# A hybrid decoder trunk on one core: gated-delta and mLSTM outputs gated by halves of the heads, weight splits moved at the starts of the feed-forward blocks

## The reference

```python
x = x + 0.5 * _rmsnorm(_swiglu(_rmsnorm(x, ng[0]), w_ffn_up[layer, 0], w_ffn_down[layer, 0]), ng[1])
h = _rmsnorm(x, ng[2])
... # h = mixer(h)
x = x + _rmsnorm(h, ng[3])
x = x + 0.5 * _rmsnorm(_swiglu(_rmsnorm(x, ng[4]), w_ffn_up[layer, 1], w_ffn_down[layer, 1]), ng[5])
```

```python
o = _rmsnorm(o, norm_w) * jax.nn.silu(z.astype(f32).reshape(B, T, GDN_HEADS, GDN_DV))   # gated delta
y = o.reshape(B, T, GDN_Z).astype(x.dtype) @ w_out
...
h = h * jax.nn.sigmoid(o.astype(f32).reshape(B, T, ML_HEADS, ML_DV))                    # mLSTM
y = h.reshape(B, T, ML_V).astype(x.dtype) @ w_out
```

## Time and profile before

| | us |
|---|---|
| median of 3 runs (lowest, highest) | 2773.89 (2772.54, 2776.75) |
| profiled execution | 2778.04 |
| its span from first to last instruction | 2776.4 |
| PE busy | 2669.9 |
| DVE, ACT, POOL busy | 1538.1, 1158.4, 287.1 |
| mean granted TensorE clock | 0.985 of full |

### The profile page before, as it was taken

One profiled execution on the slowest core, in us unless ns is written; L12 is line 12 of the kernel. 1 busy time (PEld: TensorE's weight loads), 2 busy tenths in 40 slices (PEclk: granted clock), 3 DMA queues, 4 the chain that ended last, 5 costly groups with the idle time before them and its releaser, 6 DMA issues.

```text
span 2776.4 us, 52143 instructions
## 1 busy us (share of the span) xinstructions
PE 2669.9 (96%) x22228; PEld 2518.8 (91%) x22228; DVE 1538.1 (55%) x1842; ACT 1158.4 (42%) x1571; POOL 287.1 (10%) x294
## 2 busy tenths in 40 slices
PE   7999999999999999999999999999999999999998
PEld 6998987899999986699999989699999989878998
DVE  4556744665555444465565553465455558446654
ACT  4434544444443344443344333344444335445442
POOL 1000004200200125110010000010020000042000
PEclk9999999999999999999999999999999999999999
DMA  6544522454554535444455453454455445135443
GB/s 189 164 139 147 155 81 71 152 166 146 171 166 138 194 113 160 143 146 162 144 171 166 140 177 117 126 161 163 146 169 169 141 147 166 61 99 159 153 144 101
DMA packets 415627, 404.26 MB, mean 146 GB/s; under 512 B 14786, under 2 KB 411950, under 8 KB 415086
## 3 DMA queue, kind: packets, MB, share of 16 engines
q1 hardware_dynamic: 411348, 397.42, 45.1%
q0 software_dynamic: 4096, 4.20, 0.5%
HBM read 385.19 MB, written 16.39 MB: 145 GB/s over the span
## 4 chain that ended last, share of the span: by engine, by line
PE 85%; DVE 10%; ACT 4%; issue 1%; DMA 0%; SPq 0%; ACTq 0%; DVEq 0%
PE psum L363 22%; PE psum L365 21%; PE psum L364 21%; DVE w_lo L345 2%; DVE x L574 1%; DVE y L572 1%; ACT w_hi L338 1%; PE psum L2679 1%; DVE g_cacc L1610 1%; PE psum L1150 1%; PE psum L1035 1%; PE psum L1167 1%; DVE xn_lo L499 1%; PE psum L2080 1%; PE psum L1036 1%
## 5 line engine op out<-in xcount | busy, mean ns | idle before, releaser
L345 DVE TENSOR_TENSOR w_lo<-raw,w_hi 128x2048 fp32r<-128x2048 f32 (+3 forms) x366 | 756.7, 2067 | 521.2 <-ACT w_hi L338 521.1
L363 PE MATMUL psum<-xn_hi,w_hi 128*128 128x288 f32 x3296 | 986.7, 299 | 29.9 <-DVE w_lo L345 19.1
L364 PE MATMUL psum<-xn_lo,w_hi 128*128 128x288 f32 x3296 | 977.0, 296 | 0.0
L365 PE MATMUL psum<-xn_hi,w_lo 128*128 128x288 f32 x3296 | 973.9, 295 | 0.0
L338 ACT ACTIVATE w_hi<-raw 128x2048 fp32r<-128x2048 f32 (+3 forms) x366 | 623.6, 1704 | 715.1 <-PE psum L365 672.4
L363 PEld LDWEIGHTS psum<-xn_hi,w_hi 128*128 128x128 f32 x3296 | 622.5, 189 | 41.4 <-issue 19.2
L365 PEld LDWEIGHTS psum<-xn_hi,w_lo 128*128 128x128 f32 x3296 | 625.2, 190 | 0.0
L364 PEld LDWEIGHTS psum<-xn_lo,w_hi 128*128 128x128 f32 x3296 | 623.4, 189 | 0.6
L364 PE MATMUL psum<-h_lo,w_hi 128*128 128x288 f32 x1408 | 415.5, 295 | 0.0
L363 PE MATMUL psum<-h_hi,w_hi 128*128 128x288 f32 x1408 | 415.0, 295 | 0.0
L365 PE MATMUL psum<-h_hi,w_lo 128*128 128x288 f32 x1408 | 414.9, 295 | 0.0
(11 more groups left out here) (566 smaller groups left out, 3073.3 us busy)
## 6 DMA issues: line engine op xcount, KB each, us to landing
raw<-w_ffn_up SPq DMA_DIRECT2D x176, 1024.0 KB, 5.1
raw<-w_ffn_down SPq DMA_DIRECT2D x64, 768.0 KB, 4.2
raw<-w_ffn_down SPq DMA_DIRECT2D x64, 640.0 KB, 3.9
...
```

Of the source, the lines that this page charges most:

```text
L345: dve.tensor_tensor(spread(w_lo[slot(u, i)], u), packed(raw[u % NRAW], u), spread(w_hi[slot(u, i)], u).bitcast(F32), ALU.subtract).then_in ...
L363: pe.matmul(out, wh[:, k, c], hi(k), start=st, stop=False)
L364: pe.matmul(out, wh[:, k, c], lo(k), start=False, stop=False)
L365: last = pe.matmul(out, wl[:, k, c], hi(k), start=False, stop=sp_)
```

## The change

Five edits, all of order, waits and counts; each arithmetic instruction is still there.

1. *Feed-forward start.* The split of the third unit goes ahead of the last square.
2. *Gated delta, end.* DVE gates, ACT rounds and DVE subtracts first the even parts (heads 0 to 3, chunks 0 to 3 of the projection), then the odd ones. The first unit of the projection is written out: both column halves over chunks 0 to 3, which wait for 3 `low`, then both over chunks 4 to 7, which wait for 6. The wait for `g_f` 6 is gone, and 13 fillers stand in place of 16.
3. *mLSTM, end.* The same by halves. Six updates in place of five go into the last two gate tiles, and none after them; four transposes stand ahead of the last tile and the fifth within it; three gates go between the last updates; 15 fillers are added; the copies to `nall` go behind the gates, and the transpose of `nall` and `nout` behind the first unit.
4. *mLSTM, end.* ACT waits only for the DMA of the first sample state (`l_c0_saved`), not for all four.
5. *mLSTM, start.* DVE splits the unit u0+4 within the chain of small instructions, ACT splits u0+5 ahead of its wait for that chain.

```diff
@@ act_pre_ffn
-                if k % 2 == 1:
+                if k % 2 == 1 and k < KC - 1:
                     act_square_x(act, n, k // 2)
+            act_split(act, ubase[n] + 2)
+            act_square_x(act, n, H - 1)
@@ act_ffn, pair
-                if not second:
+                if not first and not second:
                     act_split(act, u0 + 2 * j + 2, i)
@@ pe_gdn
-            pe_filled(pe, u0 + 17, 1, 16)
+            pe_filled(pe, u0 + 17, 1, 13)
             once(pe, "g_s_new", 8)
             once(pe, "g_s_odd", 8)
-            once(pe, "g_f", 6)
-            pe_out(pe, n, u0 + 17, xn(xn_hi), xn(xn_lo), lambda k: once(pe, "g_o_split", 5 + k // 4) if k % 4 == 0 else None)
+            pe.wait_ge(lo_ready, u0 + 18)
+            wh, wl = wview(w_hi[slot(u0 + 17)], u0 + 17), wview(w_lo[slot(u0 + 17)], u0 + 17)
+            for g in range(2):
+                once(pe, "g_o_split", 3 * g + 3)
+                for m in range(2):
+                    out, c = psum[:, m, 0:T], slice(m * P, (m + 1) * P)
+                    for k in range(4 * g, 4 * g + 4):
+                        pe.matmul(out, wh[:, k, c], xn_hi[:, k, :], start=k == 0, stop=False)
+                        pe.matmul(out, wh[:, k, c], xn_lo[:, k, :], start=False, stop=False)
+                        last = pe.matmul(out, wl[:, k, c], xn_hi[:, k, :], start=False, stop=k == KC - 1)
+            last.then_inc(unit_used, 1)
+            pe_out(pe, n, u0 + 17, xn(xn_hi), xn(xn_lo), None, first=1)
@@ act_gdn
-            for k in range(6):
+            for k in (0, 2, 4, 1, 3, 5):
                 hi(k)
@@ dve_gdn
             gated(0)
+            gated(2)
+            low(0)
+            gated(4)
+            low(2)
+            low(4)
             gated(1)
-            for k in range(2, 6):
-                low(k - 2)
-                gated(k)
-            low(4)
+            gated(3)
+            gated(5)
+            low(1)
+            low(3)
             low(5)
@@ sp_mlstm
-            once(sp, "l_c_out0", 64)
+            once(sp, "l_c0_saved", 16)
+            once(sp, "l_c_out0", 48)
@@ pe_mlstm
-            o_tile(pe, n, 6, range(20, 25))
-            ml_turned(pe, 0)
-            ml_turned(pe, 1)
-            o_tile(pe, n, 7, range(25, 32))
-            ml_turned(pe, 2)
-            ml_turned(pe, 3)
-            ml_turned(pe, 4)
+            o_tile(pe, n, 6, range(20, 26))
+            for k in range(4):
+                ml_turned(pe, k)
+            o_tile(pe, n, 7, range(26, 32))
+            once(pe, "l_f", 3)
+            pe_filled(pe, u0 + 13, 2, 15)
+            once(pe, "l_o_split", 3)
+            once(pe, "l_evac", 15)
...
+            last.then_inc(unit_used, 1)
             once(pe, "l_nall", 1)
-            once(pe, "l_evac", 16)
-            pe.transpose(psum[0:LH + NB * LH, 1, 0:P], nall[:], ident).then_inc(sem("l_n_turned"), 1)
-            once(pe, "l_n_out", 1)
+            pe.transpose(psum[0:LH + NB * LH, 7, 0:P], nall[:], ident).then_inc(sem("l_n_turned"), 1)
+            pe_out(pe, n, u0 + 13, xn(xn_hi), xn(xn_lo), None, first=1)
@@ act_mlstm
-                act_split(act, u0 + i + 2)
+                if i != 3:
+                    act_split(act, u0 + i + 2)
...
                 elif i == 2:
+                    act_split(act, u0 + 5)
                     once(act, "l_pre_rows", 1)
...
+            act.wait_ge(unit_used, u0 + 13)
+            for k in range(3):
+                high(k)
+            o_copy(7)
+            o_sigmoid(3)
+            for k in range(3, 6):
+                high(k)
+            once(act, "l_c0_saved", 16)
@@ dve_mlstm
                     dve.tensor_scalar(tmp4(3)[:, 0:1], tmp4(3)[:, 0:1], 0.0, None, ALU.max)
+                    dve_split(dve, u0 + 4)
                     step(dve.tensor_tensor(sq3(tmp4(3))[:, :, 0], sq3(tmp4(3))[:, :, 0], m0[:], ALU.max))
```

More of the change, by code:

```diff
@@ L575, in dve_update, with pe_out @@
             dve_enter(dve, n + 1, chunk)
-        def pe_out(pe, n, u0, hi, lo, ready):
-            for i in range(H):
+        def pe_out(pe, n, u0, hi, lo, ready, first=0):
+            for i in range(first, H):
+                if subs[n][0] == "mlstm" and i == H - 1:
+                    once(pe, "l_n_out", 1)
                 pe_unit(pe, u0 + i, [psum[:, 2 * i, 0:T], psum[:, 2 * i + 1, 0:T]], hi, lo, True, True,
@@ L1969, in pe_mlstm @@
                 ml_state(pe, h)
-            o_tile(pe, n, 6, range(20, 25))
-            ml_turned(pe, 0)
-            ml_turned(pe, 1)
-            o_tile(pe, n, 7, range(25, 32))
-            ml_turned(pe, 2)
-            ml_turned(pe, 3)
-            ml_turned(pe, 4)
+            o_tile(pe, n, 6, range(20, 26))
[6 more added lines that the diff above has]
+            once(pe, "l_evac", 15)
+            pe.wait_ge(lo_ready, u0 + 14)
+            wh, wl = wview(w_hi[slot(u0 + 13)], u0 + 13), wview(w_lo[slot(u0 + 13)], u0 + 13)
+            for g in range(2):
+                if g == 1:
+                    once(pe, "l_o_split", 6)
+                for m in range(2):
+                    if g == 0 and m == 1:
+                        once(pe, "l_evac", 16)
+                    out, c = psum[:, m, 0:T], slice(m * P, (m + 1) * P)
+                    for k in range(4 * g, 4 * g + 4):
+                        pe.matmul(out, wh[:, k, c], xn_hi[:, k, :], start=k == 0, stop=False)
+                        pe.matmul(out, wh[:, k, c], xn_lo[:, k, :], start=False, stop=False)
+                        last = pe.matmul(out, wl[:, k, c], xn_hi[:, k, :], start=False, stop=k == KC - 1)
+            last.then_inc(unit_used, 1)
             once(pe, "l_nall", 1)
-            once(pe, "l_evac", 16)
-            pe.transpose(psum[0:LH + NB * LH, 1, 0:P], nall[:], ident).then_inc(sem("l_n_turned"), 1)
-            once(pe, "l_n_out", 1)
-            pe_out(pe, n, u0 + 13, xn(xn_hi), xn(xn_lo), lambda k: once(pe, "l_o_split", 3 + 3 * (k // 4)) if k % 4 == 0 else None)
+            pe.transpose(psum[0:LH + NB * LH, 7, 0:P], nall[:], ident).then_inc(sem("l_n_turned"), 1)
+            pe_out(pe, n, u0 + 13, xn(xn_hi), xn(xn_lo), None, first=1)
         def ml_columns(pe):
@@ L2121, in ml_turned @@
             else:
-                once(pe, "l_c_new", NB * LH)
+                once(pe, "l_hs", 1)
+                once(pe, "l_f", 1)
                 for e in range(2):
-                    last = pe.transpose(psum[:, 6, tile(e)], Hs[:, tile(e)], ident)
+                    last = pe.transpose(psum[:, 4, tile(e)], Hs[:, tile(e)], ident)
             last.then_inc(sem("l_ot"), 1)
@@ L2206, in act_mlstm, with high @@
             o_copy(6)
-            o_copy(7)
-            o_sigmoid(3)
-            act.preload_act_table_set("natural_log_exp_and_others")
-            for k in range(6):
+            def high(k):
                 it, g = l_item(k)
@@ L2222, in act_mlstm @@
                 act_split(act, u0 + 13 + i + 1)
+                if i == 0:
+                    act.preload_act_table_set("natural_log_exp_and_others")
+                    once(act, "l_n_turned", 2)
+                    act.activation(nout[:], psum[0:LH + NB * LH, 7, 0:P], ACT.Copy).then_inc(sem("l_n_out"), 1)
                 act_square_y(act, n, i, u0 + 13 + i)
@@ L2338, in dve_mlstm @@
             dve_split(dve, u0 + 13)
[L2339 to L2346 removed]
+            smallT = psum[:, 4, 0:2 * P].rearrange("p (e h t) -> p h e t", e=2, h=LH)
             by_head = lambda v: v.rearrange("p (h e) t -> p h e t", e=2)
@@ L2366, in low @@
                                   ALU.subtract).then_inc(sem("l_o_split"), 1)
-            gated(0)
-            gated(1)
-            for k in range(2, 6):
-                low(k - 2)
+            updated(range(20, 26))
+            for k in range(3):
+                updated(range(26 + k, 27 + k))
                 gated(k)
-            low(4)
-            low(5)
+            updated(range(29, 32))
+            for k in range(3):
+                low(k)
+            for k in range(3, 6):
+                gated(k)
+            for k in range(3, 6):
+                low(k)
+            once(dve, "l_cpe", LH)
+            once(dve, "l_c_new", 32)
+            dve.tensor_copy(nall[:, 0:LH, None], Cp[:, :, LC:LC + 1])
+            for h in range(LH):
+                last = dve.tensor_copy(nall[:, LH:].rearrange("p (b h) -> p b h", b=NB)[:, :, h], Cin[h][:, :, LC])
+            last.then_inc(sem("l_nall"), 1)
             for i in range(H):
```

30 lines of the change are left out of this document (11 added, 19 removed).

## The result

| | before | after |
|---|---|---|
| median (runs; lowest, highest), us | 2774.99 (5; 2772.54, 2778.68) | 2758.77 (5; 2756.97, 2761.42) |
| profiled execution, us | 2778.04 | 2758.43 |
| its span, us | 2776.4 | 2756.7 |
| PE busy, us | 2669.9 | 2666.6 |
| mean granted clock | 0.985 | 0.987 |

The ratio is 0.9943, 95% interval 0.9932 to 0.9954: 15.8 us less (12.8 to 18.9). The forecast was 2755 (19.0 less), its range 2749 to 2762. Between the two profiled executions it is 19.61 us. In a later group of runs the changed kernel came to 0.9944 (0.9927 to 0.9960).

What follows compares the result with a forecast made beforehand. PE's waits, next those behind DVE's split `w_lo`, and PE's low-clock stretches were taken as the bound. Feed-forward starts 6.8, gated-delta ends 6.1, mLSTM start 4.0 and end 2.1 sum to 19.0 us: 2755, range 2749 to 2762.

Steps and rivals of the forecast that it cites:

- What bounds the kernel: Whole kernel: only PE's waits (19.1 us behind `w_lo`) and PE's stretches at the lower clock can gain; DMA none.
- Feed-forward starts, 7 x 0.97: Seven feed-forward starts: PE's third unit 1.58 us earlier, 0.6 given back waiting for the sum at L438; 6.8 in all.
- The proportional rule: Feed-forward starts: were DVE and POOL to share the port in proportion, gain near 0.9 us, almost no wait at L438.
- Gated-delta ends: Ends of both gated-delta mixers: 2.3 us each by halves, plus 1.47 for the second's low clock stretch; 6.1 in all.
- mLSTM start, 4.0: Start of the mLSTM mixer: DVE's earlier split saves PE 2.5 us, the low clock stretch behind it 1.5 more.
- mLSTM end, 2.1: End of the mLSTM mixer: 0.9 us from PE's earlier start, 1.5 from the low clock stretch, less 0.3 for L1979.
- SP's queue, 0: Feed-forward loads behind the mLSTM mixer: DMA of `n` issued 5 to 7 us later, nothing charged.
- if it took 8.8 again: DMA of `n` behind the mLSTM mixer: first feed-forward loads late by 2 to 3 us, costing about 1.3.
- a wait of ACT for `raw`: Sign of being wrong, at the feed-forward start behind the mLSTM mixer; no size given.
- the clock, 4.5 of the 19.0: Stretches near 1673, 1800 and 2514 with PE at its lower clock, about 1.5 us each, go with the waits before them.
- the clock doesn't follow: Rival: the three low clock stretches (4.5 us) come back elsewhere and the halves wait more; 2761 us, chance 0.13.
- sum in time: Rival at the seven feed-forward starts: the sum of squares isn't late, 11.1 us in place of 6.8; 2750.6, chance 0.13.

Runs made afterwards that it cites:

- the exchange alone: Kernel before with only the third unit's split put ahead of the last square at the feed-forward starts: ratio 0.9990, 2.8 us less.
- in company: Changed kernel with the feed-forward order of split and last square undone, against the kernel before: ratio 0.9971, median 2767.66 us.
- the sums cut short: Kernel before with POOL's additions of squares cut to 8 of 288 columns at seven feed-forward starts: ratio 0.9974, 7.2 us less.
- filled: Kernel before with nothing moved, its waits filled with matmuls whose result nobody reads: ratio 0.9991, median 2775.01 against 2774.94 us.

## Why the prediction was right, and where it was not

The measured 2758.8 lies within the range, 3.8 us above the forecast of 2755. Set against the kernel before in its own group, the gain is 15.8 us, and its interval (12.8 to 18.9) just leaves out the forecast 19.0.

*What bounds the kernel.* Right. The waits for `w_lo` fell from 19.1 to 6.8 us, and every place named gained.

*Feed-forward starts, 7 x 0.97.* The mechanism is right to a tenth of a microsecond: DVE 2.29 (2.27 forecast), L420 2.96 (ends at 533.66 where the count gives 1.29 after DVE), a wait of 0.51 at L438 (0.6). The proportional rule would have given almost no wait there. The Trainium skill, "SBUF — State Buffer", section "Who interferes with whom", says that the one that starts first blocks the other fully; the trace agrees (DVE 2.29, POOL's L420 done 1.29 after it), and with POOL's work cut the split fell to 2.29 in the old order too. The size in the trace is 0.9, and 6.1 over the seven starts where 6.8 was forecast. The times give 2.8 for the exchange alone and 7.7 in company, each with an interval of 3 us or more to either side.

*Gated-delta ends.* 2.3 each is right: 2.27 from gate to PE. The 1.47 for the low stretch of the second end is right for this pair of traces (3.74 in all) and wrong as a rule: of three traces with that wait of 2.06 (before, the mLSTM edits alone, the sums cut short) only the first has a low stretch behind it.

*mLSTM start, 4.0.* 4.1 in the traces (11.0 ahead to 15.13). *mLSTM end, 2.1:* 2.0 (16.75 to 18.77).

*SP's queue, 0.* I had listed "if it took 8.8 again" as what would cost 1.3. The DMA of `n` took 5.2, the load behind it 9.0, and 0.36 us were lost in one of the two profiled executions. The prediction had taken a wait of ACT for `raw` there as a sign of being wrong. It came, 1.90 and 1.39 us long, and cost almost nothing. Another such sign, low stretches at new places, came too; that is the next point.

*The step that was mis-sized* is the clock, 4.5 of the 19.0: "a low stretch thus costs 1.47 us", counted as gone for good with the wait in front. The stretches near 1673 and 1800 stand in all four traces that have both waits (before, the exchange alone, the gated-delta ends alone, the sums cut short) and in none of those where the waits are gone or filled, so the local reading was right. But the low clock over the whole program was 40.0, 40.1 and 38.7 us in the kernel before and 37.5 and 39.5 in the changed one, so 1.0 us less over all runs (39.6 over 69 runs, 38.6 over 11; -0.6 to 2.6) and not the 5.1 of three stretches. In the trace of the changed kernel three more portions stand in the second gated-delta mixer, ahead of its end, than in that of the kernel before. Without the 4.5 the sum is 14.5, and 15.8 and 15.5 were measured. So the rival "the clock doesn't follow" (2761, 0.13) holds in one half: low stretches went where they were expected to go, and about as many stood elsewhere. Its other half, that the halves wait more, is wrong: both gated-delta units take 6.66 us. The prediction also read one profile as the kernel: the first profile had three low stretches in the second gated-delta mixer, where the later traces have two to seven.

*The rival "sum in time"* fell, as the wait at L438 shows; but it named the place where the next 10 us lay.
